# The last output panel of two layers run tile by tile, with each tile's norm issued under the next tile's products

## The reference, cut to what matters

```python
def rmsnorm(x, g):
    x32 = x.astype(jnp.float32)
    y = x32 * lax.rsqrt(jnp.mean(x32 * x32, axis=-1, keepdims=True) + EPS)
    return y.astype(x.dtype) * g
...
def first_block(...):
    h = x
    for i in range(DEPTH):
        u = rmsnorm(h, norm_pre[i])
        j = i // N_MIXERS
        if i % N_MIXERS == 0:
            y = dilated_mixer(u, dil_w_in[j], dil_w_out[j])      # ends in  y @ w_out
        else:
            ...
            y = diff_mixer(u, diff_w_in[j], ..., diff_w_out[j], lambda_init)   # ends in  y @ w_out
        h = h + rmsnorm(y, norm_post[i])
    return h
```

## Time and profile before

| what | value |
|---|---|
| median of 3 runs | 2469.12 us (2468.71 to 2470.25) |
| the profiled execution's own time | 2470.61 us |
| its span in the profile | 2468.7 us |
| PE busy | 2203.0 us, 89% of the span |
| DVE, ACT, POOL busy | 944.0, 881.3, 849.3 us (38%, 36%, 34%) |
| mean granted TensorE clock | 0.946 of full speed |
| DMA traffic | 217.06 MB, mean 88 GB/s |

### The profile page before, as it was taken

How to read it: one execution, slowest core, us unless ns; L and a number is a source line. 1 busy time by engine, 2 the same in 40 slices (tenths; PEclk the granted TensorE clock), 3 DMA queues, 4 the chain that set the end, 5 groups by cost and what they waited for, 6 DMA issues and landing times. The chain is left out here.

```text
span 2468.7 us, 26092 instructions
## 1 busy us (share of the span) xinstructions
PE 2203.0 (89%) x10048; PEld 1741.3 (71%) x10048; DVE 944.0 (38%) x1627; ACT 881.3 (36%) x1800; POOL 849.3 (34%) x446
## 2 busy tenths in 40 slices
PE   4999999999957998877999999887987998999998
PEld 3877778878846776656677787675665556887876
DVE  1334334634353355643252411247553642210121
ACT  2544445655453555523231232231322312322231
POOL 3422223333323422223343344342233313444442
PEclk9999999999978999988999999898998998999999
DMA  4312122322332221112352232232223422232321
GB/s 155 97 56 69 52 70 77 95 86 69 100 142 64 94 69 52 52 47 98 103 150 90 86 79 93 68 100 68 82 81 126 146 95 77 86 103 85 103 92 62
DMA packets 129483, 217.06 MB, mean 88 GB/s; under 512 B 8633, under 2 KB 58345, under 8 KB 129153
## 3 DMA queue, kind: packets, MB, share of 16 engines
q1 hardware_dynamic: 110720, 168.63, 22.2%
q0 software_dynamic: 7952, 28.40, 3.5%
q10 hardware_dynamic: 10688, 18.35, 2.1%
HBM read 197.24 MB, written 17.52 MB: 87 GB/s over the span
## 5 line engine op out<-in xcount | busy, mean ns | idle before, releaser
L2277 POOL TENSOR_TENSOR lo_ring<-raw_ring,hi_ring 128x1024 fp32r<-128x1024 f32 (+1 forms) x304 | 730.3, 2425 | 1179.9 <-ACT hi_ring L1926 1179.8
L882 PE MATMUL bank<-xh,hi_ring 128*128 128x512 f32 x1472 | 601.2, 408 | 5.3 <-DVE xl L1366 3.2
L882 PE MATMUL bank<-xh,lo_ring 128*128 128x512 f32 x1472 | 582.0, 395 | 0.0
L882 PE MATMUL bank<-xl,hi_ring 128*128 128x512 f32 x1472 | 581.2, 395 | 0.0
L1926 ACT CAST hi_ring<-raw_ring 128x1024 fp32r<-128x1024 f32 (+1 forms) x304 | 303.2, 1044 | 508.4 <-PE bank L882 489.2
L882 PEld LDWEIGHTS bank<-xh,hi_ring 128*128 128x128 f32 x1472 | 282.4, 192 | 76.8 <-issue 18.3
L882 PEld LDWEIGHTS bank<-xh,lo_ring 128*128 128x128 f32 x1472 | 281.1, 191 | 61.6
L882 PEld LDWEIGHTS bank<-xl,hi_ring 128*128 128x128 f32 x1472 | 282.4, 192 | 58.1 <-issue 2.6
L882 PE MATMUL bank<-hi_ring,xh 128*128 128x512 f32 (+1 forms) x608 | 252.3, 415 | 16.5 <-POOL lo_ring L2277 6.3
L882 PE MATMUL bank<-hi_ring,xl 128*128 128x512 f32 (+1 forms) x608 | 244.6, 402 | 0.0
L882 PE MATMUL bank<-lo_ring,xh 128*128 128x512 f32 (+1 forms) x608 | 244.6, 402 | 0.0
(11 more groups left out here) (245 smaller groups left out, 2489.8 us busy)
## 6 DMA issues: line engine op xcount, KB each, us to landing
raw_ring<-in_ffn_w_in SPq DMA_DIRECT2D x176, 256.0 KB, 3.1
raw_ring<-in_dil_w_in SPq DMA_DIRECT2D x80, 512.0 KB, 3.6
raw_ring<-in_ffn_w_out SPq DMA_DIRECT2D x44, 512.0 KB, 3.8
raw_ring<-in_diff_w_in SPq DMA_DIRECT2D x32, 512.0 KB, 3.5
raw_ring<-in_w_in SPq DMA_DIRECT2D x32, 512.0 KB, 3.6
arena<-scratch_heads POOLq DMA_DIRECT2D x4, 1584.0 KB, 13.8
scratch_gates<-arena ACTq DMA_DIRECT2D x24, 256.0 KB, 2.0
arena<-scratch_gates POOLq DMA_DIRECT2D x24, 256.0 KB, 3.9
```

Source lines behind the costliest of these rows:

```text
L882: ins = T.matmul(bank[pb][:, 0:S if p.form == "feature" else p.cols], lhsT, rhs, start=(k == 0 and m == 0), stop=(k == p.K - 1 and m == le ...
L2277: G.tensor_tensor(lo, raw_ring[:, p % RAW, 0:q.kq * q.n], hi.bitcast(F32), ALU.subtract).then_inc(lowered, 1)
```

## The change

Each engine has the same work instructions as before. Their order, the homes of some weight pieces and some waits differ.

1. *Panel y1 by tile* (both layers). Its `mac` jobs go in the order `BY_TILE`: both steps into bank 4, then both into bank 5, and so on. So all four of its pieces must be split and stay: they get homes of their own, `wide_a` (three pieces) and `wide_b` (one), in parts of the arena that hold nothing else at that time. The look-ahead is larger: step 1 of y0 splits six pieces past its own, the steps of y1 six and four.
2. *Norms under products.* `square_y`, `scale_y`, `add_y`, `norm_scale`, `norm_tile` and `lower` of tile n stand between the `mac` jobs of tiles n+1 and n+2. The banks for the transposes are now (4, 4, 6, 4).
3. *Layer 0 only: V panel behind it.* The first three `mac` jobs of the differential layer's V panel stand among the jobs of tiles 2 and 3, and V runs in the order `BY_HALF` (banks 0 and 1 through both steps, then banks 2 and 3). A bank waits for its own row tile. The barrier at the end of layer 0 is gone; `lambda` is split into `lambda_in` (load) and `lambda`, which now stands behind the q panel.
4. *Heads in a row.* Heads 4 to 7 are weighed before y0; each is turned and lowered behind one `mac` of y0's step 0.

```diff
+WIDE_AT = 6144, 14336
...
-            self.steps.append(Step(pi, pieces, first, last, end, len(self.pieces) + 2))
-            for b in range(4):
+            m = first // (2 * KP)
+            self.steps.append(Step(pi, pieces, first, last, end, len(self.pieces) + look[m], look_at[m]))
+            for b in range(4 if order is None else 0):
                 self.job("mac", s, b)
                 yield MAC_TIME if parted else RAW_TIME
...
+        for m, b in order or ():
+            self.job("mac", len(self.steps) - K // (2 * KP) + m, b)
+            yield MAC_TIME if parted else RAW_TIME
...
-    for c in range(first, 2):
-        run_all(plan.panel("y", w, c * 512, 512, "tile", at=(c,), base=4 * c))
-    plan.job("scale_y", 0)
-    for n in range(NT + 2):
-        if n < NT:
-            if n + 1 < NT:
-                plan.job("scale_y", n + 1)
-            plan.job("add_y", n)
-            plan.job("norm_scale", n, None)
-        if 1 <= n <= NT:
-            plan.tile_parts("norm_tile", n - 1)
-        if n >= 2:
-            plan.job("lower", n - 2)
+        run_all(plan.panel("y", w, 0, 512, "tile", at=(0,), look=(2, 6)))
+    main = plan.panel("y", w, 512, 512, "tile", at=(1,), base=4, wide=True, look=(6, 4), order=BY_TILE)
...
+    products(main, 2)
+    plan.job("square_y", 0)
+    add(0)
+    plan.job("norm_scale", 0, None)
+    for n in (1, 2):
+        products(main, 2 if n == 1 else 1)
+        plan.job("square_y", n)
+        products(main, 1)
+        turn(n - 1)
+        add(n)
+        lower(n - 1)
+        plan.job("norm_scale", n, None)
+    products(main, 1)
+    plan.job("square_y", 3)
+    if following is None:
+        turn(2)
+        add(3)
+        plan.job("norm_scale", 3, None)
+        lower(2)
+        turn(3)
+        lower(3)
+        plan.job("gain", next_name)
+        plan.job("over", False)
+        return
+    needs = [plan.parts[0], plan.parts[1], (), ()]
+    behind = following(plan, needs)
+    products(behind, 1)
+    turn(2)
+    add(3)
+    lower(2)
+    plan.job("norm_scale", 3, None)
+    products(behind, 2)
+    turn(3)
+    lower(3)
+    needs[2:] = plan.parts[2:]
     plan.job("gain", next_name)
-    plan.job("over", False)
+    run_all(behind)
...
+    for h in range(4, 8):
+        plan.job("o_weigh", h)
     plan.parts = (sum(ready, ()),) * NT
     late = [(), (), (), ()]
-    main = plan.panel("y", "diff_w_out", 0, 512, "tile", at=(0,), late=late)
-    for _ in range(4):
-        next(main)
+    main = plan.panel("y", "diff_w_out", 0, 512, "tile", at=(0,), late=late, look=(2, 6))
     ready = []
     for h in range(4, 8):
-        plan.job("o_weigh", h)
+        next(main)
         ready.append(turn_head(h))
         plan.job("o_lower", h)
```

More of the change, by code:

```diff
@@ L84 @@
 Panel = namedtuple("Panel", "kind at n w cols K form src use needs base late")
-Step = namedtuple("Step", "panel pieces k0 last end ahead")
-Piece = namedtuple("Piece", "w k0 kq c0 n parted split step halves landed")
+Step = namedtuple("Step", "panel pieces k0 last end ahead look_at")
+Piece = namedtuple("Piece", "w k0 kq c0 n parted split step halves landed home prior")
 class Plan:
@@ L112, in job, with piece, panel @@
         return use
-    def piece(self, w, k0, kq, c0, n, parted, halves):
+    def piece(self, w, k0, kq, c0, n, parted, halves, wide=None):
         slot = len(self.pieces) % RAW
         self.slot_landed[slot] += 16 * halves
-        self.pieces.append(Piece(w, k0, kq, c0, n, parted, self.n_split, len(self.steps), halves, self.slot_landed[slot]))
+        home, prior = None, None
+        if parted and wide is None:
+            home = self.n_ring % SPLIT
+            prior, self.last_of[home] = self.last_of[home], len(self.steps)
+            self.n_ring += 1
+        elif parted:
+            home = SPLIT + wide
+        self.pieces.append(Piece(w, k0, kq, c0, n, parted, self.n_split, len(self.steps), halves, self.slot_landed[slot], home, prior))
         self.n_split += 1 if parted else 0
         return len(self.pieces) - 1
-    def panel(self, kind, w, c0, cols, form, at=(), K=KC, src="x", k_first=0, halves=1, after=(), base=0, late=((),) * 4):
+    def panel(self, kind, w, c0, cols, form, at=(), K=KC, src="x", k_first=0, halves=1, after=(), base=0, late=((),) * 4,
+              wide=False, look=(2, 2, 2), look_at=(0, 0, 0), order=None, needs=None):
         parted = src in ("x", "hidden")
@@ L134, in panel @@
             s, last = len(self.steps), first + 2 * KP >= K
-            pieces = [self.piece(w, k_first + k, min(KP, K - k), c0, cols, parted, halves) for k in (first, first + KP) if k < K]
+            pieces = [self.piece(w, k_first + k, min(KP, K - k), c0, cols, parted, halves, k // KP if wide else None)
+                      for k in (first, first + KP) if k < K]
             if last:
@@ L204, in norm_to_parts, with finish_layer @@
         if n >= 2:
-            plan.job("lower", n - 2)
+            plan.job("lower", n - 2, 4 + 2 * (n % 2))
     plan.job("gain", next_name)
-def finish_layer(plan, w, row_name, next_name, first=0):
+BY_TILE = [(m, b) for b in range(4) for m in range(2)]
+BY_HALF = [(m, b) for pair in ((0, 1), (2, 3)) for m in range(2) for b in pair]
+TURN_BANKS = (4, 4, 6, 4)
+def finish_layer(plan, w, row_name, next_name, following, first=0):
     if first == 0:
@@ L212, in finish_layer, with turn, add, lower @@
         plan.job("row", row_name)
[L213 to L225 removed]
+        run_all(plan.panel("y", w, 0, 512, "tile", at=(0,), look=(2, 6)))
+    main = plan.panel("y", w, 512, 512, "tile", at=(1,), base=4, wide=True, look=(6, 4), order=BY_TILE)
+    def turn(n):
+        plan.tile_parts("norm_tile", n, TURN_BANKS[n])
+    def add(n):
+        plan.job("scale_y", n)
+        plan.job("add_y", n)
+    def lower(n):
+        plan.job("lower", n, TURN_BANKS[n])
+    def products(stream, n):
+        for _ in range(n):
+            next(stream)
+    products(main, 2)
[33 more added lines that the diff above has]
+    needs[2:] = plan.parts[2:]
     plan.job("gain", next_name)
[L227 removed]
+    run_all(behind)
 def gate_panels(plan, w, c0, layer):
@@ L396, in before_hybrid @@
             end = ("stepped", plan.n_step)
-        plan.steps.append(Step(None, [p], first, last, end, len(plan.pieces)))
+        plan.steps.append(Step(None, [p], first, last, end, len(plan.pieces), 0))
         plan.job("mem_kv", s, use)
@@ L643, in program @@
         jobs, panels, steps, pieces, use_of = plan.jobs, plan.panels, plan.steps, plan.pieces, plan.use_of
-        split_of = [q for q in pieces if q.parted]
         filled = [sem(f"filled{b}") for b in range(8)]
```

74 lines of the change are left out of this document (46 added, 28 removed).

## The result

The changed kernel takes 2428.2 us (median of four, 2424.3 to 2436.7) where the kernel before takes 2469.7: a ratio of 0.984, 95% interval 0.9825 to 0.9853. Forecast were 2431 us and 2424 to 2445. Timed again with the experiments it took 2428.9 (ratio 0.9835, 0.9812 to 0.9858).

What follows compares the result with a forecast made beforehand. PE, busy 89% of the span, was taken as the bound. Savings of 19.1 + 11.2 + 7.8 = 38.1 us off the profiled 2470.6 give 2432.5; the median, 1.5 lower, was forecast at 2431 us, range 2424 to 2445.

Steps and rivals of the forecast that it cites:

- the slow start: First feed-forward matmuls after layer 1's tail: PE restarts at the lower clock after idling, taken as 1.6 us lost.
- Layer 0, 19.1 us: End of y1 to end of V in layer 0: 44.9 us become 25.8, saving 19.1 us.
- The cover of 0.9 us for q's second piece: Layer 0, start of q: second piece ready at 5.9 us, PE wants it at 6.8; any excess shows once.
- Layer 1, heads, 11.2 us: y0 of layer 1, heads turned between macs: 28.0 us against 39.2, saving 11.2 us.
- Layer 1, y1 and tail, 7.8 us: y1 and tail of layer 1: 35.6 us against 45.0, 9.4 saved, less 1.6 for a slow restart.
- the 0.6 us of stall in y1: Layer 1, turn of tile 0: PE reaches it at 1106.8 but bank 5 comes free at 1107.7, 0.6 us stall.
- Rival A: End of layer 1: POOL's queue of lowerings bounds, delaying tile turns; 5 to 7 us, about 2437 us; chance 0.14.
- Rival B: Row tiles: cycle longer than 6.4 us, at 7.8 PE waits at six turns; 11 us, 2443 us; chance 0.10.
- Rival C: Run of turns: waits above about 3.5 us lower the clock for y1 and V; slower, 2489 us; chance 0.03.
- Rival D: y1's second step, both layers: waits for pieces held back by SP's raw slots; 8.7 us, 2440 us; chance 0.05.

## Why the prediction was right

**The time.** 38.1 us were summed up for the three places and 37.7 were found in stretches A and B. That they lie within 0.4 is in part luck, as the misses inside layer 1's last term (a stall that did not occur, slower matmuls, a shorter tail, a dearer restart) nearly cancel. The medians differ by 41.5 (40.6 in the second set of runs), 3 to 4 us more, which no term of mine has. In the profiles the surplus is spread over unchanged code, and the hybrid stage alone varied by 10.5 us. I had forecast the first feed-forward matmul 38 to 41 us earlier; it is 43.3. The cost of the slow start lies behind it, and 3.0 us were gained in unchanged code ahead of it.

**Layer 0, 19.1 us.** Measured 19.2. The turns were forecast at 759.0, 765.4, 771.8 and 778.3 and stand 1.5 to 1.6 us earlier, as the stage itself begins 1.75 earlier. `norm_tile(0)` starts at 754.33 for 1.28 us and PE turns it at 757.42, so the slack is 1.8 us (forecast 2.0). Of the 19.2, V under the tail is 9.4 and the turns under the products are 3.0, by the two kernels that undo them one after the other. The other 6.8 belong to what no kernel undid alone, the order by tile with squares, sums and powers under it. The cover of 0.9 us for q's second piece held: it is cast from 785.98 on, as V's step 0 ends, and PE waits for no lowering there.

**Layer 1, heads, 11.2 us.** Measured 11.1, as y0's 39.2 us became 28.1, and 11.1 again by undoing it. The first turn waited 0.5 (forecast 0.6) and step 1 waited 1.77 (forecast 1.9). Moving the last turn gave back 2.0, so that wait cost hardly more than itself, as I had assumed of the clock.

**Layer 1, y1 and tail, 7.8 us.** 7.4 are left of B's 18.5. y0 took 28.1 us and y1 24.3, against 28.0 and 24.4. But the 0.6 us of stall in y1 did not occur: `norm_tile(0)` started at 1083.22 and bank 5 was free at 1085.36, both just in time for a turn at 1085.04 whose second half comes half a microsecond later. In its place y1's matmuls are slower, by 0.6 us a panel (last section). The tail is 10.7 instead of 11.2, and the slow start cost more: from the first feed-forward matmul to the end of B it is 39.39 us against 36.87 in the kernel before, 2.5 us where I had taken 1.6. This is the term that was mis-sized, within the bound of 2.7 that I had given it.

**Rival A** (POOL's queue) did not happen, but its mechanism is real. The last four lowerings of the run of eight and the small sum and power of tile 0, in the changed kernel's timeline of layer 1:

```profile
1069.49 9.50 POOL L2356 TENSOR_TENSOR lo_ring<-raw_ring,hi_ring 128x1024 fp32r<-128x1024 f32 x4
1077.62 1.39 DVE L1455 TENSOR_TENSOR small<-small 128x1 f32<-128x1 f32 x1 [4.47 <-ACT arena L2081]
1079.27 0.57 POOL L2364 TENSOR_TENSOR small<-small,minus_half 128x1 f32<-128x1 f32 x1 [0.28 <-DVE small L1457]
```

The sum was held up by 1.2 us, and PE's turn had 0.5 us left. Two lowerings left behind the first powers brought the rival's mechanism at once: 4.5 us in layer 0. I had priced it by lowerings that come late ahead of tile 0. The place where it bit is tile 3 of layer 0, and the look-ahead in the change, to which I gave no term of its own, is what averts it there.

**Rival B** (a longer tile cycle) is refuted: the turns are 6.4 to 6.5 us apart, at PE's pace. **Rival C** (the clock falls at each turn) too: granted clock 1.00 over y1 and V of layer 0. But its condition, a wait of more than about 3.5 us at a turn, was set too high: the one wait of 2.65 us with the last two pieces late lowered the clock. **Rival D** did not happen, though what prevents it has its price: 2.1 us a layer when the casts of y1's last pieces stand behind the squares of y0, and 16.6 us in all without wide homes and with the shorter look-ahead that goes with them.

## What to carry to other kernels

A chain of small operations between two products hides if the panel before it is finished tile by tile, but then every queue that the chain passes must be empty when it comes. Move long background work (here lowerings of 2.4 us) ahead of it, even where it isn't urgent, and look at in-order queues, not at busy shares. Where nothing independent follows, cut the dependent product by the same tiles as the chain: 256 columns ran at 0.12 us against 0.227 for 512, so the cut cost 1.2 us, and the stretch still became 7.5 shorter. Compare variants by fixed stretches of the profile where the total varies by more than the edit.

## What the chip showed that I had not expected

A VectorE operation on one column with two SBUF inputs, 0.15 us long, took 1.39 us in layer 1 above, until POOL's lowering ended at 1079.0. With the look-ahead of two it took 2.26:

```profile
750.07 4.79 POOL L2356 TENSOR_TENSOR lo_ring<-raw_ring,hi_ring 128x1024 fp32r<-128x1024 f32 x2
...
752.62 2.26 DVE L1455 TENSOR_TENSOR small<-small 128x1 f32<-128x1 f32 x1 [7.48 <-ACT arena L2081]
```

It ends at 754.88, as POOL's instruction does (754.86). By the Trainium skill's page "SBUF — State Buffer", section "SBUF: two separate sides", the two hold one pair of ports by turns for a whole instruction. The trace agrees: in both places a DVE instruction of 0.15 us ended within 0.03 us of POOL's. So even the smallest one on a critical chain can wait for a whole lowering of 2.4 us.

Matmuls that read y1's weights from the wide homes start 0.233 us apart, those from the ring 0.227. Three of them (one of each product) in y1 of layer 0 of the changed kernel take 0.70 us:

```profile
766.16 0.63 PE L961 MATMUL bank<-wide_b,xh 128*128 128x512 f32 x2
766.63 0.39 PE L961 MATMUL bank<-wide_b,xl 128*128 128x512 f32 x1
766.86 0.63 PE L961 MATMUL bank<-wide_b,xh 128*128 128x512 f32 x2
```

and 0.68 in y1 of layer 1 of the kernel with ring homes, in the same order by tile:

```profile
1087.26 0.39 PE L961 MATMUL bank<-hi_ring,xh 128*128 128x512 f32 x1
...
1087.94 0.39 PE L961 MATMUL bank<-hi_ring,xh 128*128 128x512 f32 x1
```

With a look-ahead of two, which keeps the wide homes, it is 0.70 again (769.66 to 770.36). So it is where the weights lie, not the order or the look-ahead, and 16 macs lose some 1.2 us by it. Why the place matters was not tried.

How long PE may wait before it restarts at the lower clock isn't told by the wait alone. In the changed kernel a matmul behind 1.77 us of waiting took 0.47 us and its successors 0.39 to 0.40, at the upper level. In the kernel before, 1.76 us in the same place were followed by 0.76; there PE had already waited 2.6 us at each of three heads. With the last two pieces late a single 2.65 us, behind matmuls without a gap, was enough, though 3.12 us in the earlier trace rows were not. And the feed-forward matmul behind 1.60 us took 0.76 in the changed kernel and 0.47 in the kernel before, although the tail before held more idle time. What differs is the stretch just ahead. In the kernel before, two turns stand close together there and the clock is back up at the matmul; these are its windows before and behind that point:

```profile
1140.00:1149.30 9.30, 4.20 (x18) 0.60 0.16 52
1149.37:1159.00 9.63, 9.63 (x43) 1.00 0.32 95
```

In the changed kernel one turn stands there, behind 4.55 us of waiting, and the clock is at 0.50 for the next 5.4 us:

```profile
1106.00:1111.40 5.40, 5.30 (x13) 0.50 0.39 122
```

No run here shows which of these things decides.
